# First weight unit of a three-layer transformer kernel on the unnormalized input, its norm's factor applied where its tiles are read

## What is computed

```python
mem_n = rms_norm(mem, mem_norm_w)              # memory, 256 rows
h = rms_norm(x, ln1_w[l])                      # x: 512 x 1024
proj = h @ w_in[l]                             # 1024 x 2560
xr = proj[..., :D_RNN]                         # 512 columns: tiles 0 to 3
xg = proj[..., D_RNN:2 * D_RNN]                # then the gelu gate, q, k, v
xc = conv(xr, conv_w) + conv_b                 # 4 taps in time, each channel alone
r = sigmoid(xc @ w_a + b_a);  i = sigmoid(xc @ w_x + b_x)

def rms_norm(x, w):
    return x * rsqrt(mean(x * x, axis=-1) + EPS) * w
```

## Time and profile before

| | |
|---|---|
| median of 3 runs | 2410.89 us (2410.87 to 2411.92) |
| the profiled execution: its own time | 2413.93 us |
| its span | 2411.8 us |
| TensorE busy | 2195.8 us (91%) |
| VectorE busy | 1584.2 us (66%) |
| ScalarE busy | 1187.5 us (49%) |
| share of TensorE in the chain that ended last | 76% |
| mean granted TensorE clock | 0.957 |

### The profile page before, as it was taken

One profiled execution on the slowest core, in us unless ns is written; L12 is line 12 of the kernel. 1 busy time (PEld: TensorE's weight loads), 2 busy tenths in 40 slices (PEclk: granted clock), 3 DMA queues, 4 the chain that ended last, 5 costly groups with the idle time before them and its releaser, 6 DMA issues.

```text
span 2411.8 us, 27159 instructions
## 1 busy us (share of the span) xinstructions
PE 2195.8 (91%) x10362; PEld 1741.0 (72%) x10362; DVE 1584.2 (66%) x1884; ACT 1187.5 (49%) x1437; POOL 205.1 (9%) x155
## 2 busy tenths in 40 slices
PE   6998898889999999993988989999989798999997
PEld 4786577677777787772855778888766466888885
DVE  6447543468888888885677476465568767655565
ACT  4535533357777777775466342222245554322223
POOL 1000000021111111110010011020100100211020
PEclk9998899989999999996999999999999999999998
DMA  5242031469999999975210113223222002232321
GB/s 193 91 151 97 18 123 35 179 162 362 357 359 350 356 363 357 351 290 213 73 52 17 53 70 105 88 88 107 103 87 70 36 1 76 100 105 83 109 88 53
DMA packets 48814, 359.98 MB, mean 149 GB/s; under 512 B 12224, under 2 KB 13416, under 8 KB 21456
## 3 DMA queue, kind: packets, MB, share of 16 engines
q1 hardware_dynamic: 36880, 340.89, 38.5%
q0 software_dynamic: 10752, 13.60, 1.7%
q10 hardware_dynamic: 1088, 4.19, 0.4%
HBM read 360.71 MB, written 25.72 MB: 160 GB/s over the span
## 4 chain that ended last, share of the span: by engine, by line
PE 76%; DVE 11%; ACT 8%; issue 4%; DMA 1%; ACTq 0%; SPq 0%; DVEq 0%; POOLq 0%
PE bank L1031 40%; PE bank L498 14%; PE bank L1942 10%; DVE split_products L562 3%; ACT split_products L726 2%; PE bank L1967 2%; PE bank L1744 1%; PE bank L488 1%; PE bank L1729 1%; ACT S L1808 1%; PE bank L1758 1%; DVE X L1282 1%; DVE split_weights L1237 1%; ACT S L1819 1%; ACT S L761 1%
## 5 line engine op out<-in xcount | busy, mean ns | idle before, releaser
L1031 PE MATMUL bank<-split_x_high,split_weights 128*128 128x512 f32 x2144 | 672.5, 394 | 31.2 <-DVE split_x_low L1251 14.7
L1245 ACT ACTIVATE split_weights<-ring 128x2048 fp32r<-128x2048 f32 (+1 forms) x122 | 228.2, 1872 | 648.2 <-PE bank L1031 526.5
L1031 PEld LDWEIGHTS bank<-split_x_high,split_weights 128*128 128x128 f32 x2144 | 407.8, 190 | 122.2 <-issue 36.8
L1237 DVE TENSOR_TENSOR split_weights<-ring,split_weights 128x2048 fp32r<-128x2048 f32 (+1 forms) x122 | 276.6, 2268 | 228.5 <-ACT split_weights L1245 228.4
L1031 PE MATMUL bank<-split_products,split_weights 128*128 128x512 f32 x1200 | 334.4, 395 | 4.5 <-DVE split_products L1437 4.5
L1031 PE MATMUL bank<-split_x_low,split_weights 128*128 128x512 f32 x800 | 312.5, 391 | 0.0
L1031 PEld LDWEIGHTS bank<-split_products,split_weights 128*128 128x128 f32 x1200 | 229.0, 191 | 53.9 <-DVE split_products L1437 6.0
L498 PE MATMUL bank<-split_products 128*128 128x512 f32 x768 | 189.7, 396 | 11.8 <-DVE split_products L562 11.8
L498 PE MATMUL bank<-split_x_low,split_products 128*128 128x512 f32 x768 | 192.4, 400 | 6.8 <-DVE split_x_low L562 4.7
L498 PE MATMUL bank<-split_x_high,split_products 128*128 128x512 f32 x768 | 190.0, 397 | 8.0 <-DVE split_x_high L562 8.0
L562 DVE TENSOR_TENSOR split_products<-ring,split_products 128x2048 fp32r<-128x2048 f32 x63 | 144.4, 2293 | 57.9 <-ACT split_products L726 52.8
(11 more groups left out here) (421 smaller groups left out, 2973.4 us busy)
## 6 DMA issues: line engine op xcount, KB each, us to landing
ring<-in_expert_down_w SPq DMA_DIRECT2D x32, 2048.0 KB
ring<-in_expert_gate_w SPq DMA_DIRECT2D x31, 2048.0 KB, 8.3
ring<-in_expert_up_w SPq DMA_DIRECT2D x31, 2048.0 KB, 7.8
ring<-in_ffn_w_up SPq DMA_DIRECT2D x44, 1024.0 KB, 4.8
ring<-in_w_in SPq DMA_DIRECT2D x26, 1024.0 KB, 4.9
ring<-in_ffn_w_down SPq DMA_DIRECT2D x16, 1024.0 KB, 4.7
ring<-in_w_out SPq DMA_DIRECT2D x12, 1024.0 KB, 4.8
ring<-in_ffn_w_down SPq DMA_DIRECT2D x8, 768.0 KB, 4.1
```

What stands on the lines that cost most here:

```text
L1031: mm = pe.matmul(acc[:, :], w[:, u, k, m], x, start=first and q == 0, stop=last and q == 2)
L1237: st.tell(dve.tensor_tensor(w[:, 1, 0:ks, 0:nc_], raw_half(g)[:, :, 0:nc_], as_f32(w[:, 0, 0:ks, 0:nc_]), ALU.subtract), wl_done)
L1245: st.tell(act.activation(WHL[g % 2][:, 0, 0:ks, 0:nc_], raw_half(g)[:, :, 0:nc_], ACT.Copy), wh_done)
```

## The change

Unit 0 is multiplied with the input times the norm's weight only, `XH0 + XL0 = X * ln1`, without the token's factor. These parts lie in `QP`, which is free then. ScalarE writes `XH0` (Identity with the weight as scale) and VectorE `XL0` as soon as X is there. The statistic's matmuls move into the middle of unit 0, ahead of its chunk 4. Unit 0's weights are split in two halves of four chunks, and TensorE starts when the first half is ready. The factor is applied by VectorE, which reads tiles 0 and 1 out of their banks and multiplies them by `rstd`; ScalarE's evacuation of these two is gone. Unit 1 and all later ones still use the normed input. Unit 2's halves are made in the midst of the normed chunks: the high one after `high` of chunk 3, the low one after chunk 5. `cols` is loaded behind the first piece of X, `konst` behind unit 0; waits and counts follow.

```diff
-            sp.dma_start(konst[:, :], A["konst"]).then_inc(s_const, 16)
-            sp.dma_start(cols[:, :], A["cols"]).then_inc(s_const, 16)
+                if i == 0:
+                    sp.dma_start(cols[:, :], A["cols"]).then_inc(s_cols, 16)
...
+                if g == 0:
+                    sp.dma_start(konst[:, :], A["konst"]).then_inc(s_const, 16)
...
-            pe.wait_ge(s_const, 32)
...
-            rms("ln1", ((a_add, 5, LN1[0]), (a_sq, 7, LN1[6]), (a_sq, 8, LN1[7])))
+            def first_chunk(k):
+
+                if k == 0:
+                    pe.wait_ge(first_half, 2)
+                if k == DC // 2:
+                    pe.wait_ge(s_const, 16)
+                    rms("ln1", ((a_add, 5, LN1[0]), (a_sq, 7, LN1[6]), (a_sq, 8, LN1[7])))
+                    pe.wait_ge(wl_done, 1)
+                pe.wait_ge(a_lo, k + 1)
+
+            xraw = (lambda k: XH0[:, k, :], lambda k: XL0[:, k, :])
...
-            split_unit(0, **tiles(0), count=xin, before=lambda k: pe.wait_ge(a_lo, k + 1), together=True)
-            split_unit(1, **tiles(2), count=xin)
+            split_unit(0, **tiles(0), count=xraw, before=first_chunk, together=True)
+            split_unit(1, **tiles(2), count=xin, before=lambda k: pe.wait_ge(a_lo, DC + k + 1), together=True)
...
+            dve.wait_ge(s_cols, 16)
+            for c in range(DC):
+                dve.wait_ge(a_hi, c + 1)
+                st.tell(dve.scalar_tensor_tensor(XL0[:, c, :], X[:, c, :], col("ln1", c), as_f32(XH0[:, c, :]), ALU.mult, ALU.subtract), a_lo)
+            add_ln1(1, 4)
+            dve.wait_ge(first_half, 1)
+            st.tell(dve.tensor_tensor(WHL[0][:, 1, 0:4, :], raw_half(0)[:, 0:4, :], as_f32(WHL[0][:, 0, 0:4, :]), ALU.subtract), first_half)
+            dve.wait_ge(wh_done, 1)
+            st.tell(dve.tensor_tensor(WHL[0][:, 1, 4:8, :], raw_half(0)[:, 4:8, :], as_f32(WHL[0][:, 0, 4:8, :]), ALU.subtract), wl_done)
+            add_ln1(4, 6)
             unit_low(dve, st, 1)
...
-            normed_split(0, 0, DC, lambda c: X[:, c, :], lambda c: col("ln1", c), lambda c: HN[:, c, :],
-                         lambda c: (XL[:, c, :], as_f32(XH[:, c, :])))
+            normed_split(0, DC, DC, lambda c: X[:, c, :], lambda c: col("ln1", c), lambda c: HN[:, c, :],
+                         lambda c: (XL[:, c, :], as_f32(XH[:, c, :])), lambda c: unit_low(dve, st, 2) if c == 5 else None)
+            for c in range(2):
+                dve.wait_ge(tile_done, c + 1)
+                st.tell(dve.tensor_tensor(XR[:, c, :], bank[c][:, :], rstd[:, :], ALU.mult), tile_free)
+            st.wait()
...
-            unit_low(dve, st, 2)
             conv(0)
             conv(1)
...
+            act.wait_ge(s_cols, 16)
             for c in range(DC):
                 act.wait_ge(s_x[c // 2], 16)
+                st.tell(act.activation(XH0[:, c, :], X[:, c, :], ACT.Identity, scale=col("ln1", c)), a_hi)
+            for c in range(DC // 2):
                 st.tell(act.activation(LN1[c], X[:, c, :], ACT.Square), a_sq)
-            unit_high(act, st, 0)
+            act.wait_ge(half_landed[0], 16)
+            st.tell(act.activation(WHL[0][:, 0, 0:4, :], raw_half(0)[:, 0:4, :], ACT.Copy), first_half)
+            st.tell(act.activation(WHL[0][:, 0, 4:8, :], raw_half(0)[:, 4:8, :], ACT.Copy), wh_done)
+            for c in range(DC // 2, DC):
+                st.tell(act.activation(LN1[c], X[:, c, :], ACT.Square), a_sq)
             unit_high(act, st, 1)
...
                 high(c + 1, XH[:, c, :], HN[:, c, :])
-
-            n = [0]
+                if c == 3:
+                    unit_high(act, st, 2)
+
+            n = [2]
...
-            unit_high(act, st, 2)
-            for c in range(2):
-                evac(XR[:, c, :], full)
             act.wait_ge(s_mem, 16)
             st.tell(act.activation(MSQ, MT, ACT.Square), side_act)
             unit_high(act, st, 3)
+            act.wait_ge(tile_free, 2)
             for c in range(2, 4):
                 evac(XR[:, c, :], full)
```

More of the change, by code:

```diff
@@ L175, in build @@
         MSUM, MRSTD = S[:, 20, 0:MEM], S[:, 21, 0:MEM]
+        XH0, XL0 = QP[:, 0:DC, :], QP[:, DC:2 * DC, :]
         LN1, HN = [S[:, c, :] for c in range(DC)], S[:, 8:16, :]
@@ L179, in build @@
         add_base = {2 * DC: 10, 3 * DC: 16}
-        s_const = sem("const_landed")
+        s_const, s_cols, first_half = sem("const_landed"), sem("cols_landed"), sem("first_unit_half")
         s_x = [sem(f"x_or_y_landed{i}") for i in range(4)]
@@ L694, in moe_vector @@
                 unit_low(dve, st, UA + g)
-            dve.wait_ge(s_const, 48)
+            dve.wait_ge(s_const, 32)
             for t in range(TT):
@@ L1929, in split_unit @@
             def split_unit(g, n0, done, free, count, n=T, before=None, order=tuple(range(DC)), together=False):
-                pe.wait_ge(wl_done, g + 1)
+                if g:
+                    pe.wait_ge(wl_done, g + 1)
                 w = WHL[g % 2]
@@ L2022, in _ @@
             mixed = (lambda k: MIX[:, k, :], lambda k: MIXL[k])
-            split_unit(18, **res(0), count=mixed, before=lambda k: pe.wait_ge(a_lo, DC + k + 1), together=True)
+            split_unit(18, **res(0), count=mixed, before=lambda k: pe.wait_ge(a_lo, 2 * DC + k + 1), together=True)
             for u in range(1, 4):
@@ L2028, in _ @@
             pe.wait_ge(res_free, 8)
-            split_unit(22, **tiles(A_XQ), count=xq, before=lambda k: pe.wait_ge(a_lo, 2 * DC + k + 1), together=True)
+            split_unit(22, **tiles(A_XQ), count=xq, before=lambda k: pe.wait_ge(a_lo, 3 * DC + k + 1), together=True)
             for u in range(1, 4):
@@ L2059, in add_square, with add_ln1, normed_split @@
                 st.tell(dve.tensor_tensor(SUM if m != 1 else SUM, first if m == 1 else SUM, nxt, ALU.add), a_add)
[L2061 to L2065, removed]
+            def add_ln1(a, b):
+                for m in range(a, b):
+                    dve.wait_ge(a_sq, m + 1)
+                    st.tell(dve.tensor_tensor(LN1[0], LN1[0], LN1[m], ALU.add), a_add)
+                    st.wait()
[9 more added lines that the diff above has]
+            add_ln1(4, 6)
             unit_low(dve, st, 1)
-            def normed_split(stat, before, chunks, src, w, dst, lo, order=None):
+            def normed_split(stat, before, chunks, src, w, dst, lo, between=None):
                 def low(c):
@@ L2079, in normed_split @@
                         low(c - 1)
+                    if between:
+                        between(c)
                 low(chunks - 1)
-            dve.wait_ge(s_const, 32)
-            normed_split(0, 0, DC, lambda c: X[:, c, :], lambda c: col("ln1", c), lambda c: HN[:, c, :],
-                         lambda c: (XL[:, c, :], as_f32(XH[:, c, :])))
+            dve.wait_ge(s_const, 16)
+            normed_split(0, DC, DC, lambda c: X[:, c, :], lambda c: col("ln1", c), lambda c: HN[:, c, :],
[3 more added lines that the diff above has]
+                st.tell(dve.tensor_tensor(XR[:, c, :], bank[c][:, :], rstd[:, :], ALU.mult), tile_free)
+            st.wait()
             def conv(c):
@@ L2173, in inside @@
                     c = p - 4
-                    dve.wait_ge(a_hi, DC + c + 1)
+                    dve.wait_ge(a_hi, 2 * DC + c + 1)
                     st.tell(dve.tensor_tensor(MIXL[c], G[:, c, :], as_f32(MIX[:, c, :]), ALU.subtract), a_lo)
@@ L2181, in _ @@
             dve_pairs(dve, st, att_cfg[0], 0, inside)
-            normed_split(2, DC + HC, HC, lambda c: S[:, 12 + c, :], lambda c: col("gn_att", c), lambda c: S[:, 12 + c, :],
+            normed_split(2, 2 * DC + HC, HC, lambda c: S[:, 12 + c, :], lambda c: col("gn_att", c), lambda c: S[:, 12 + c, :],
                          lambda c: (MIXL[4 + c], as_f32(MIX[:, 4 + c, :])))
@@ L2198, in _ @@
             residual(0, 2 * DC, 20)
-            normed_split(3, 2 * DC, DC, lambda c: X[:, c, :], lambda c: col("ln2", c), lambda c: HN[:, c, :],
+            normed_split(3, 3 * DC, DC, lambda c: X[:, c, :], lambda c: col("ln2", c), lambda c: HN[:, c, :],
                          lambda c: (SP[:, c, :], as_f32(XH[:, c, :])))
@@ L2249, in _ @@
             unit_high(act, st, 3)
+            act.wait_ge(tile_free, 2)
             for c in range(2, 4):
                 evac(XR[:, c, :], full)
-            act.wait_ge(s_const, 32)
             lam = cols[:, C1["lam"]:C1["lam"] + HC]
```

## The result

The changed kernel takes 2416.51 us, the median of 20 runs, against 2411.23 us for 20 runs of the kernel before. The ratio is 1.0021 with a 95% interval of 1.0014 to 1.0028: slower by 5.1 us, between 3.4 and 6.8. Single runs of one kernel spread over 6 to 9 us, so that a total tells less here than an instant in a trace. But a trace is one execution, and instants vary too: over the seven traces here in which X was loaded in the same way as in the changed kernel, its last piece landed between 12.3 and 14.1 us. A difference of less than 1 us between two traces is therefore read step by step, not from one instant. The profiled span is 2416.2 us, 4.4 more than before.

The account below looks back on a forecast made before the run. TensorE bounds the kernel; unit 2's start hangs on VectorE's reduction of the memory's squares. A reduction later by +0.5 us and a clock price of +3.0 give +3.5 on the median 2410.89: 2414.4 us, range 2408.5 to 2418.5.

Parts of the forecast that it names:

- (a): Whole kernel: the prediction's own forecast, slower by +1.5 to +4.8 us; chance 0.55.
- (c): Statistic in unit 0 late by over 1.3 us beyond 27.0: slower by over 0.2%, up to +8.1 us; chance 0.23.
- unit 0 starts: TensorE's first product: at 16.25 us where it started at 25.76, 9.5 us gained.
- 24 products: Unit 0's products ahead of the statistic: 13.5 in 5.75 us at the low clock, 10.5 more in 2.4.
- reduction ends: End of VectorE's list ahead of unit 2: at 53.85 us, +0.5 us against the kernel before.
- price of the clock in unit 2: Unit 2 starts at the low clock after TensorE's longer idle: +3.0 us.
- Loads: Start of the kernel: `cols` costs later X pieces 0.2 us, at most 1.2; last X piece at 10.1 us.
- Root: ScalarE before the first normed chunk: table load over by 21.4 us, only the statistic waited for; root 6.2 us later.
- Clock: TensorE: falls in some 8.7 us of idle before unit 2; rises 5.75 us after a start from rest.
- Stall, factor, hidden work: Normed chunks to unit 2: low(4) waits 0.75 us, two multiplications add 1.3, unit_high(2) and unit 1's stall cost nothing.
- signs of a wrong forecast: Trace: short wait at line 1986, unit 2 in 10.9 us, or statistic over before 24 or after 29 us.
- (d): Line 1986 does not hold TensorE, unit 2 follows unit 1: -8.2 us, 2402.7; chance 0.07.

Follow-up runs that it names:

- gatew_late: Changed kernel with GpSimd's four gate-weight loads held until the last piece of X is there; ratio 1.0016 to the kernel before.
- gap_and_three: Changed kernel with reduce_in_gap, load_ahead, gatew_late and stat_at_2 together; 2400.19 us, ratio 0.9954 to the kernel before.
- cols_behind: Changed kernel with `cols` loaded behind the fourth piece of X instead of behind the first; ratio 1.0021 to the kernel before.
- load_ahead: Changed kernel with ScalarE's wait for the four eps columns moved ahead of the first half, one wait left before the first Ln; ratio 1.0032 to the kernel before.
- reduce_first: Changed kernel with VectorE's reduction ahead of the factor's two multiplications and the convolutions; ratio 1.0005 to the kernel before.
- stat_at_2: Changed kernel with the statistic's three matmuls ahead of chunk 2 instead of chunk 4; ratio 1.0009 to the kernel before.
- low2_behind: Changed kernel with VectorE's low half of unit 2 behind the normed chunks instead of after chunk 5; ratio 1.0021 to the kernel before.
- reduce_in_gap: Changed kernel with ScalarE's squares of the memory and VectorE's reduction moved into the gap where both wait for the statistic; ratio 0.9980 to the kernel before.
- before_reduce_first: Kernel before with VectorE's reduction of the memory's squares put ahead of conv(0); ratio 0.9982 to the kernel before.
- before_two: Kernel before with its reduction ahead of conv(0) and the gate weights loaded behind X; ratio 0.9975 to the kernel before.

## Why the prediction came out as it did

The forecast was 2414.4 us, +3.5, "same"; the measured ratio is +5.1 us with an interval from 3.4 to 6.8, so the forecast of +3.5 lies at its lower end and the measured time within the range. Read by the bands of the rivals, +5.1 is just beyond (a), which ended at +4.8 and had the chance of 0.55, and in (c), "slower by over 0.2%", with 0.23; the interval covers both. The mechanism was the right one: the reduction at the end of VectorE's list, delayed by the statistic in the middle of unit 0, and the clock lost in TensorE's longer idle. Its terms, in the prediction's order:

| step | forecast | profile after | moved by |
|---|---|---|---|
| unit 0 starts | 16.25 | 19.11 | +2.9 |
| 24 products | 8.15 | 7.40 | -0.75 |
| statistic's three matmuls | 2.6 | 2.6 | 0 |
| its end to the first normed chunk | 2.73 | 4.10 | +1.4 |
| normed chunks with unit 2's low half | 13.5 | 13.3 | -0.2 |
| factor on two tiles | 1.3 | 1.24 | 0 |
| convolutions and reduction | 9.34 | 9.22 | -0.1 |
| reduction ends | 53.85 | 56.96 | +3.1 |
| price of the clock in unit 2 | 3.0 | 1.5 | -1.5 |

**Loads: mis-sized.** I let `cols` cost X 0.2 us with 1.2 as the most, from what `cols` had cost when it stood last. In front, together with the gate weights, the last piece of X came 2.9 us later than forecast, at 13.04. gatew_late, gap_and_three and cols_behind show that these two loads are the reason, and that unit 0's load alone is not. The bound was taken from a row in which the same bytes stood behind X, and it left out that `cols` delays the issue of the later pieces by 0.5 us. My reason for the 0.2, small packets of other queues in that stretch, does not hold either: the gate weights' packets are of 4096 B. The other links from X to TensorE's start were a little off one by one (VectorE's three sums and not the high half were the last to be ready), but their sum was right: 6.15 us in the forecast, 6.07 in the trace.

**Root: a wrong step.** "Now the load is over by 21.4 and only the statistic is waited for": it was not; it stood behind the wait and cost 1.28 us. load_ahead shows that this hangs on the second wait in front of the first Ln. In the kernel before, the same two waits stood there, but the statistic was over at 18.4, before ScalarE came to them, so the row I read could not show it. (The Trainium skill, "ScalarE: Activation LUTs", "Step-by-step: what each stage is for", says that the compiler places the load right before the activation that needs it; the trace agrees, and adds that a separate wait can stand ahead of both.)

**Clock: mechanism right, size half.** The fall in the idle came as forecast (0.50 in 54 to 56), but the rise came sooner after the new start (start at 57.01, rise at about 60.2; before, start at 25.76, rise at about 31.8, by the 0.60 of the window 31 to 32): unit 2 and the row sum lost 1.5 us, not 3.0, and unit 2 took 11.89 us and not some 14. The same sum at the first products was 0.75 too long. Both prices vary with the run: 24 products took 7.10 to 8.50 us in these traces, and unit 2 took 11.75 to 12.50 in the six that waited 8 to 10 us ahead of it, so that the price with the row sum's 0.5 was 1.3 to 2.1, in none of them 3.0. And idle of 2.5 us did not keep the clock in reduce_first, which my row of 2.8 us had suggested. On the level at the start the granted clock and the pace disagree: the changed kernel's windows read 1.00 from 12 us on, while 24 products took 7.40 us instead of 5.47, and in stat_at_2 the first 12 took 0.46 us each, half the full pace. (The pace agrees with the rule that I weighed, of the Trainium skill, "TensorE: Matmul & The Clock Gate", "What's actually happening", that the throttled state is the default; the 1.00 does not.)

**Stall, factor, hidden work: right.** The stall before low(4) was 0.50 us (0.75 forecast), the multiplications 1.24, unit 2's high half did not wait for unit 0, and unit 1's stall cost nothing (low2_behind).

**The rivals.** (c), a late statistic, is in the main what happened: it was over at 29.10 against my 27.0, 2.1 late where the threshold was 1.3. But it was late from X (+2.9), and not from the clock of the 24 products, the one place that I had named; that came out 0.75 better. The table load added its 1.3 behind the statistic. It also meets one of my own signs of a wrong forecast, the statistic over after 29. (d) did not happen by itself. reduce_in_gap removed the wait, and the row sum then started at 49.19, 4.2 us earlier than in the kernel before and not 8.2. In the sum two errors of opposite sign, +3.1 for the start of the row sum and -1.5 for the clock, partly cancelled and left it 1.6 us short: that the forecast came so close is luck as far as these two go.

## What to carry to other kernels

An early start of the bounding engine is worth only what the next wait in its list lets through: look first for the last wait before the engine becomes steady, and at what stands ahead of it on the other engine. Here a reduction that could have been done much earlier stood at the end of a list. Up to the end of unit 2, moving it ahead of the convolutions was worth 3.6 us in the trace of the kernel before, and moving it into the gap 9.6 in that of the changed one. Work that an engine does for a later stage belongs into the gap in which it waits for a result, and a statistic that many wait for belongs ahead of long products (12 products fewer ahead of it: 1.7 us).

## What the runs showed of the hardware

- With 48 KB of `cols` behind the first of four 512 KB pieces on one queue and 256 KB of gate weights on another, the last piece landed at 12.3 to 14.1 us (seven traces). With `cols` behind the pieces it landed at 9.9 to 10.5 (before, before_reduce_first, cols_behind), with the gate weights held back at 10.9 (gatew_late, gap_and_three), with both at 9.1 (before_two).
- A table load stood behind the second of two waits that preceded its activation (29.17, the statistic over at 29.10), and ahead of the wait when there was only one (23.33, load_ahead): 1.28 us on the path. In cols_behind it ran at 4.48, ahead of the first of two waits, which ended at 11.63.
- The granted clock fell after idle stretches of 2.5 and 0.6 us in reduce_first, after TensorE had begun again, and stayed through one of 2.8 us in the kernel before.
- The granted clock read 1.00 while the first products ran at half the pace: 12 in 5.49 us in stat_at_2, 48 in 10.93 us later.
